# Three slots in place of five for the first block's weights, the two set free going to expert matrices

## The reference, cut to what matters

```python
def first_block(x, mem, ...):
    h = rms_norm(x, mix_norm_g[l])
    u_pool, q_down, kv_down, k_rope_in, xq, gate_logits = split(h @ w_in[l])
    y_pool, y_mla, y_mem = pool_mixer(...), mla_branch(...), memory_cross_attention(...)
    gates = jax.nn.sigmoid(gate_logits.reshape(B, S, N_BRANCHES, D) + gate_b[l])
    merged = (gates[:, :, 0] * (y_pool @ w_br_pool[l])
              + gates[:, :, 1] * (y_mla @ w_br_mla[l])
              + gates[:, :, 2] * (y_mem @ w_br_mem[l]))
    x = x + merged @ w_out[l]
    h2 = rms_norm(x, ffn_norm_g[l])
    x = x + hierarchical_moe(h2, ..., w_gate_e[l], w_up_e[l], w_down_e[l])
    return rms_norm(x, final_norm_g)
```

## Time and profile before

| | |
|---|---|
| runs | 783.73 us median of 3 (783.34 to 784.84) |
| profiled execution | span 782.0 us, first to last instruction |
| PE busy | 735.6 us, 94% |
| DVE, ACT busy | 419.5 us (54%), 335.4 us (43%) |
| DMA | 203.97 MB, mean 261 GB/s |
| chain that ended last | PE 86%, DMA 8%, ACT 3%, DVE 2% |

### The profile page before, as it was taken

How to read it: one execution, slowest core, us unless ns; L and a number is a source line. 1 busy time by engine, 2 the same in 40 slices (tenths; PEclk the granted TensorE clock), 3 DMA queues, 4 the chain that set the end, 5 groups by cost and what they waited for, 6 DMA issues and landing times.

```text
span 782.0 us, 12563 instructions
## 1 busy us (share of the span) xinstructions
PE 735.6 (94%) x5192; PEld 608.0 (78%) x5192; DVE 419.5 (54%) x747; ACT 335.4 (43%) x603; POOL 30.0 (4%) x64
## 2 busy tenths in 40 slices
PE   8999999999999999998766889999999999999997
PEld 8898888888788876665543559999878888888885
DVE  4758746667667421110100207766658776777675
ACT  6766565454444421110110117566556534344433
POOL 0700000000000000000000001100001000000001
PEclk9999999999999999999988999999999999999999
DMA  8762567347968899999999998963424464555201
GB/s 309 287 256 95 196 248 267 124 175 266 360 229 335 345 395 422 420 421 419 421 421 421 421 416 326 408 222 137 162 109 148 146 244 162 176 201 178 92 1 54
DMA packets 32010, 203.97 MB, mean 261 GB/s; under 512 B 3792, under 2 KB 4176, under 8 KB 9936
## 3 DMA queue, kind: packets, MB, share of 16 engines
q1 hardware_dynamic: 31952, 203.15, 66.9%
HBM read 202.09 MB, written 1.05 MB: 260 GB/s over the span
## 4 chain that ended last, share of the span: by engine, by line
PE 86%; DMA 8%; ACT 3%; DVE 2%; issue 1%; SPq 1%; DVEq 0%; POOLq 0%; POOL 0%; ACTq 0%
PE ps L658 45%; PE ps L727 10%; DMA ext<-in_w_up_e 7%; PE ps L1022 6%; PE ps L730 5%; PE ps L999 3%; PE ps L1057 2%; PE ps L1047 2%; PE ps L777 2%; PE ps L1149 1%; PE ps L1163 1%; PE ps L1177 1%; PE ps L621 1%; ACT wh L1309 1%; ACT big L1560 1%
## 5 line engine op out<-in xcount | busy, mean ns | idle before, releaser
L1720 DVE TENSOR_TENSOR wl<-raw,wh 128x1024 fp32r<-128x1024 f32 (+3 forms) x180 | 213.2, 1200 | 129.6 <-ACT wh L1309 128.4
L1309 ACT CAST wh<-raw 128x1024 fp32r<-128x1024 f32 (+3 forms) x180 | 182.0, 1029 | 63.2 <-PE ps L658 44.0
L658 PE MATMUL ps<-wh,fra 128*128 128x512 f32 (+3 forms) x668 | 189.4, 369 | 0.4 <-DVE gb L1934 0.4
L658 PEld LDWEIGHTS ps<-wh,fra 128*128 128x128 f32 x668 | 118.7, 189 | 19.2 <-issue 1.0
L658 PE MATMUL ps<-wl,fra 128*128 128x512 f32 (+3 forms) x334 | 121.5, 364 | 0.0
L727 PE MATMUL ps<-fra,wh 128*128 128x512 f32 x352 | 110.7, 396 | 0.7 <-DVE fra L1731 0.7
L730 PEld LDWEIGHTS ps<-fra,wl 128*128 128x128 f32 x352 | 66.1, 188 | 15.5
L658 PE MATMUL ps<-wh,frb 128*128 128x512 f32 x240 | 74.4, 391 | 0.0
L658 PE MATMUL ps<-fra,wh 128*128 128x256 f32 x400 | 73.8, 286 | 0.1
L658 PEld LDWEIGHTS ps<-wl,fra 128*128 128x128 f32 x334 | 62.9, 188 | 9.6
L730 PE MATMUL ps<-fra,wl 128*128 128x256 f32 x352 | 69.3, 278 | 0.0
(11 more groups left out here) (269 smaller groups left out, 938.7 us busy)
## 6 DMA issues: line engine op xcount, KB each, us to landing
raw<-in_dense SPq DMA_DIRECT2D x79, 1024.0 KB, 5.0
raw<-in_w_gate_e SPq DMA_DIRECT2D x25, 1024.0 KB, 26.0
ext<-in_w_up_e SPq DMA_DIRECT2D x24, 1024.0 KB, 26.1
ext<-in_w_down_e SPq DMA_DIRECT2D x16, 1024.0 KB, 23.5
raw<-in_dense SPq DMA_DIRECT2D x16, 512.0 KB, 7.1
big<-in_w_up_e SPq DMA_DIRECT2D x8, 1024.0 KB, 20.7
raw<-in_w_down_e SPq DMA_DIRECT2D x4, 1024.0 KB, 19.6
gb<-in_w_down_e SPq DMA_DIRECT2D x4, 1024.0 KB, 20.8
```

The costliest lines, as they stand in the source:

```text
L658: t = e.matmul(o, a, w, start=first and n == 0, stop=final and n == 2, skip_group_check=not check)
L1309: e.copy(halves(q)[0], piece_view(q)).then_inc(*up("wh", q))
L1720: e.tensor_tensor(l, piece_view(q), h.bitcast(F), ALU.subtract).then_inc(*up("wl", q))
```

## The change

```diff
-DENSE = 5
+DENSE = 3
@@ plan
-        ring = ([(RAW - 1, None)] + [(self.slot[u], u) for u in apart] + [(RAW + EXT + z, None) for z in (1, 2, 3)]
+        ring = ([(z, None) for z in range(DENSE + len(apart), RAW)] + [(self.slot[u], u) for u in apart] + [(RAW + EXT + z, None) for z in (1, 2, 3)]
                 + [(RAW + z, None) for z in (8, 9)] + left[:1] + [(RAW + EXT + BIG, None)]
@@ sync, expert(n)
-            if n == 3:
+            if n == 5:
                 e.wait_ge(*at("values", "m", 7))
...
@@ sync
         expert_at = {first_unit(*key) + k: n for n, (key, k) in enumerate((
-            (("uv", 0), 0), (("gate", 2, 0), 0), (("gate", 2, 0), 1), (("gate", 1, 1), 1), (("br", 1, 0), 0),
+            (("uqn", 0), 0), (("uqn", 1), 0), (("uv", 0), 0), (("gate", 2, 0), 0), (("gate", 2, 0), 1), (("gate", 1, 1), 1), (("br", 1, 0), 0),
             (("br", 1, 0), 1), (("br", 1, 1), 1), (("out", 0), 0), (("out", 1), 2)))}
-        for u in range(DENSE, wt.dense_end):
+        for u in range(5, wt.dense_end):
...
-        for n in range(9, wt.expert_end - wt.dense_end):
+        for n in range(11, wt.expert_end - wt.dense_end):
```

More of the change, by code:

```diff
@@ L534, in expert @@
         def expert(n):
-            if n == 3:
+            if n == 5:
                 e.wait_ge(*at("values", "m", 7))
-            if n == 6:
+            if n == 8:
                 e.wait_ge(*at("piece", last["br", 2, 1]))
-            if n == 9:
+            if n == 11:
                 e.wait_ge(*at("merged", 4, 1))
                 e.wait_ge(*at("biased", 5, 1))
-            if n == 10:
+            if n == 12:
                 e.wait_ge(*at("piece", last["br", 1, 1]))
```

## The result

| | before | after |
|---|---|---|
| runs, median of 4 | 784.29 us (783.34 to 785.33) | 795.95 us (795.04 to 796.20) |
| ratio | | 1.0142, 95% interval 1.0130 to 1.0154 |
| profiled execution, span | 782.0 us | 794.3 us |

The change costs 11.7 us in the runs, 12.3 us between the two profiled executions. Forecast were +7.2 us and at most +9.5; so the direction and the place of the greater part were right. The size was too small, and a fifth of the loss sits at the start, where the prediction had put nothing.

What follows compares the result with a forecast made beforehand. TensorE was taken to bound until about 275 us, DMA from about 284 to 455, then TensorE; 0 + 0 + 0 + 5.2 + 2.0 = +7.2 us gave runs of 790.9 us, forecast 789.0 to 793.2 (65%), range 786.2 to 793.2.

Steps and rivals of the forecast that it cites:

- two early matrices: Before the DMA-bound experts' stage: two expert matrices, 2.1 MB, loaded early gain nothing; term 0.
- start: First loads: x, sent some 5 us later, lands at most 0.8 us later; term 0, bound +0.8.
- dense weights: Gates: with three slots each 1 MB unit still lands before its first split; term 0.
- bias 4 late: Gate 5: bias 4 lands at 212.5, 5.2 us late, and TensorE waits; +5.2 us, bounds +4.9 and +5.6.
- clock after it: Behind the stall at gate 5: TensorE restarts at a lowered clock; +2.0 us.
- the one from the release of the slots: Before the first refill: the load into the output weights' slot waits until 246 us; last slot lands 283.4 to 284.8.
- the hole just behind the first refill: 280 to 285 us: DMA moves 336 GB/s, not 421, a hole of 1.0 us; earlier loads lengthen it.
- The sign that would have counted against the term: Experts' stage: less time than now from first refill to end of last expert would prove the prediction wrong.
- The rival in which the early matrices pay: Experts' stage: 5.0 us come off, 778.7 us without the stall, 785.9 with it; chance 4%.
- Bias 3: Gates: sent behind the split at 188.25, lands at 193.7, 2.8 us late; delays VectorE's later splits and thereby unit 39.
- The small load overtakes: Gate biases: small loads land before earlier weights, bias 4 lands at 206.2, no stall, 783.7 us; chance 6%.
- more than one stall: An early bias or the first gate unit also stalls TensorE, or the clock stays low longer; +9.5 to +12, 8%.

Runs made afterwards that it cites:

- 3: Changed kernel with all six gate-bias loads two units earlier and the first five dense units sent without a wait; 785.94 us, ratio 1.0019 against the kernel before.
- 8: Changed kernel with the first four dense units sent without a wait and all gate biases two units earlier; 785.46 us, ratio 1.0017 against the kernel before.
- 2: Changed kernel with only its first five dense units sent without a wait, three slots from there on; 794.57 us, ratio 1.0118 against the kernel before.
- 9: Kernel before, five slots, with only units 3 to 7 waiting for the split three units ahead; 786.89 us, ratio 1.0039 against the kernel before.
- 5: Changed kernel with only the load of bias 3 two units earlier; 792.27 us, ratio 1.0085 against the kernel before.
- 7: Changed kernel with the load of x ahead of the fifth unit's fetch; 798.87 us, ratio 1.0170 against the kernel before.
- 4: Kernel before, five slots, with only bias 4 and the router's weights loaded three units later; 795.06 us, ratio 1.0122 against the kernel before.
- 6: Changed kernel with only bias 4 and the router's weights loaded one unit earlier; 788.20 us, ratio 1.0038 against the kernel before.

## Why the prediction was wrong in size and right in kind

| term | predicted | measured |
|---|---|---|
| two early matrices | 0 | 0.1 in the trace of after, no gain in 3 and 8 |
| start | 0, bound +0.8 | +2.6 (1.2 to 2.7 with the same start) |
| dense weights | 0 | 0: no split in the gates waited for its unit |
| bias 4 late | +5.2 (4.9 to 5.6) | +7.1 |
| clock after it | +2.0 (1.7 to 2.3) | +2.5 |
| sum | +7.2 | +12.3 |

**The early matrices: the term right, one of its two arguments wrong.** The argument that held is the one from the release of the slots: in 3 the load from which the prediction counted is sent at 246.39, and the last of the 24 slots lands at 284.75, within the predicted 283.4 to 284.8. The load whose slot is freed last sets this moment, and two loads sent at 69 and 75 us don't move it. In after this slot (sent at 284.73, 12.1 us under way) lands at 296.8, 3.7 us behind the first refill, before 3.1. The argument that did not hold is the hole just behind the first refill. It was to grow, and it closed: from 280 to 285 us the kernel before moves 336 GB/s at a DMA share of 0.92, and 3 moves 367 at 0.99. The sign that would have counted against the term, less time from the first refill to the last expert, came by 0.8 us in after (184.5), but not in 2 and 3 (185.3), and far short of 5.0. The rival in which the early matrices pay had its chance at 4%, and fell.

**The start: the step that failed.** The prediction saw that x is under way for 11.3 us, took from this that the queue is full, and concluded that a load sent 5 us later still finds it nearly full. The 11.3 us were a backlog: seven loads, 3.25 MB, sent between 2.1 and 6.1 us, were still under way when x was sent. The change delays the last two of these, the fourth and the fifth unit (from 5.14 to 9.04 and from 6.11 to 10.92), so the backlog shrinks with them. At 9.04, when the fourth unit is sent, 2.1 us of queue are left (the last piece of `mem` lands at 11.13). A measure of the queue before the change was used for the queue after it. x landed 3.9 us later (21.81 against 17.90), where the bound was 0.8. And the slack was asked of x, while the link that broke is the sixth unit behind it. The term was 2.6 us in place of 0. Runs 9 (alone, +1.9) and 2 and 8 (mended, shift 0.14 and 0.16) show it by itself.

**Bias 4: the mechanism right, the size short by 1.9.** Each step can be laid beside the trace of after, 2.6 us being taken off for the start.
- Bias 3 was to be sent at 188.65 and was (191.27 - 2.6). It was given 5.1 us and took 6.1: the row used for it had one fetch ahead, while now unit 36 is sent at 187.81 and unit 37 at 190.89, 3.1 us apart, and both are still under way when bias 3 is sent. It was 3.8 us late and not 2.8.
- The split of piece 61 and unit 39 carried this on unchanged, as predicted: sent at 204.8 (207.42 - 2.6) and not 203.8. Run 5 shows this link: with bias 3 in time it is gone, and 3.5 us of the gap with it.
- Bias 4 was to land 8.7 us behind the issue of unit 39 and landed 9.7 behind it (217.14 - 207.42). Unit 39 took 5.0 and the expert's matrix 2.5 more, as counted; the difference is the bias itself, 1.9 us behind the router's weights (208.34 + 6.9 to 208.74 + 8.4), where 0.6 to 1.3 was taken. In 2, 5 and 7 these 1.9 us stand again. In all four a load of 1 MB is sent about 1 to 2 us behind the bias (209.69 in after). In 4, where nothing is sent for 14 us behind the bias, it landed 0.6 behind the router's weights, which speaks for that load as the cause; but 9 has 0.6 too, with a load sent 5.5 us behind the bias, and the kernel before 1.3. It stays open.
- Biases 0 to 2 were late by at most 1.6 us (bias 2 landed at 177.31, used at 177.33) and TensorE saw nothing of it, as predicted.

The sum of the two single microseconds, 5.2 + 1.0 + 1.0 = 7.2, is the measured 7.1.

**The clock: right, short by 0.5.** The granted clock fell to 0.50 (1.2 GHz) in the stall, and returned 4.9 us after the restart. Of the Trainium skill (TensorE: Matmul & The Clock Gate, Part 1) the sentence that was weighed holds: an idle array falls to 1.2 GHz and returns only after work; by a reading without it the stall would have cost 7.1 and not 9.6.

**The rivals.** "The small load overtakes" is out: in every trace each bias landed behind what had been sent ahead of it. The Trainium skill (DMA: Bandwidth & Descriptors, Queues, rings and completion order) allows a later transfer to finish earlier; by the profile's landings none of the 221 transfers did in any of the twelve traces. The case nearest to the measured number was "more than one stall" (+9.5 to +12, 8%). That is in part luck: the second stall is real, but it sits at 28 us, at neither of the places that this rival names (an early bias, the first gate unit), and the clock stayed low for only 0.3 us longer than the 4.6 of the prediction.

**The range.** Its lower end does not follow from the terms: 4.9 + 1.7 us give 790.3 us and not 789.0. The upper end does, within 0.1 (5.6 + 2.3 + 0.8 + 0.7 = 9.4). The miss adds up as 7.2 as forecast, 2.6 for the start, 1.9 more for bias 4 and 0.5 more for the clock: 12.2, of 12.3 measured.

## What to carry to other kernels

Fewer buffers in a ring delay not only the loads that use it but everything that stands behind their waits on the same issuing engine; look for the small load with its own buffer and no cover, and move it ahead of the wait (one place in the queue was worth 8 us here). When a change takes away early issues, the latencies of the old trace hold a backlog that goes with them: count the bytes in the queue at the new time of issue. Loading earlier for the stage that DMA bounds brought nothing here, since neither the release of its last slots nor the first refill came sooner; ask of such a change whether one of these moves.

## What the runs showed of the hardware

**The cost of the clock is not in proportion to the stall.** The same place of the program, with TensorE's gap varied by the place of one or two small loads:

| kernel | gap us | clock loss us | granted clock behind it |
|---|---|---|---|
| 6 | 1.1 | 0.0 | 1.00 |
| 5 | 4.0 | 1.6 | 0.70 in 215 to 220 |
| 2 | 7.4 | 2.5 | 0.50 in 215 to 220, 0.98 in 220 to 225 |
| 7 | 7.4 | 3.0 | 0.50 in 215 to 220, 0.55 in 220 to 225 |
| after | 7.5 | 2.5 | 0.50 in 215 to 220, 0.71 in 220 to 225 |
| 4 | 9.0 | 1.9 | 0.50 in 215 to 220, 0.94 in 220 to 225 |

The longest stall lost less clock than the shorter ones. What the loss goes with is how long the clock stayed at 0.50 behind the restart. By these rows that is 3.4 us in 5, 4.1 in 4, 4.7 in 2 and 4.9 in after and 7; half of it is 1.7, 2.0, 2.4, 2.5 and 2.5, near the measured loss in all but 7. And a gap of 1.75 us at 28 us was followed, in 6, by a clock of 0.67 in the next stretch, where a gap of 1.51 us at the same place of after had none (TensorE was busy for 2.25 us of the four from 26 to 30 in 6, and 2.49 in after). Why the one lost its clock and the other not, these rows don't tell.

**A load sent alone is slow.** Between 100 and 230 us a unit of 1 MB took 4.7 to 5.1 us from issue to landing when nothing stood ahead of it (four of 106 over all traces took 5.2 to 5.9); sent in a row, further ones came 2.5 us apart. In the start of after the fifth unit, sent 1.9 us behind the fourth with x right behind it, landed 5.3 us after it; sent in a row with five slots, 2.5 us after it.
